# A two-layer diffusion step on one core: filter products over all 128 rows, two sample tiles routed by pairs, sample rows squared ahead

## What is computed

```python
def _rmsnorm(x, g):
    return x * rsqrt(mean(x * x, axis=-1) + EPS) * g

h = _rmsnorm(x, norm_mix) * (1 + scale1) + shift1        # first norm of a layer

f = sin(z @ w1 + b1); f = sin(f @ w2 + b2)               # implicit filters
h = (f @ w3)                                             # w3 has 64 rows
filt = h * exp(-decay * t)

q = (h2 @ wq)                                            # 8 heads, two halves each
s = einsum(q, sub_keys)                                  # 128 scores for each half
s1, i1 = top_k(s[:, :, 0], 16); s2, i2 = top_k(s[:, :, 1], 16)
cand = s1[..., :, None] + s2[..., None, :]               # routing
top, pos = top_k(cand, 16); g = softmax(top)
a = gelu(einsum('td,thkd->thk', h2, u_tab[idx]))         # 128 experts for each row
x = x + gate2 * einsum('thk,thkd->td', a * g, v_tab[idx])
```

## Time and profile before

| what | us |
|---|---|
| median of 3 runs | 4684.39 |
| the three runs | 4674.54 to 4685.51 |
| the profiled execution's own time | 4676.89 |
| its span | 4675.1 |

### The profile page before, as it was taken

The page is one execution under the profiler, slowest core; times in us unless marked ns, Lnnn a source line. Parts: engine busy times, 40 slices in busy tenths (PEclk is TensorE's granted clock), DMA queues, the critical chain, the costliest instruction groups (busy, mean ns, idle before and its releaser), DMA issues.

```text
span 4675.1 us, 42187 instructions
## 1 busy us (share of the span) xinstructions
PE 3775.7 (81%) x12598; PEld 2021.8 (43%) x12598; DVE 3207.1 (69%) x7383; ACT 1562.2 (33%) x4531; POOL 2083.7 (45%) x1769
## 2 busy tenths in 40 slices
PE   7988799897897877757867789999698777777776
PEld 4547574446453333324533356446554232332222
DVE  1322878887888876766567778977798866755554
ACT  2321341001344444434334333100234444444444
POOL 2240355573344434454444455565244444444443
PEclk8889899998899998988999899999899899899999
DMA  7655478896899989999999777877699999999998
GB/s 278 203 203 221 178 243 299 309 348 227 330 419 401 406 364 402 417 412 386 390 420 421 299 276 271 318 279 270 268 412 409 388 410 422 408 417 421 422 421 346
DMA packets 268416, 1604.74 MB, mean 343 GB/s; under 512 B 31686, under 2 KB 34034, under 8 KB 112540
## 3 DMA queue, kind: packets, MB, share of 16 engines
q0 software_dynamic: 234880, 1395.89, 75.3%
q1 hardware_dynamic: 33308, 206.16, 11.3%
HBM read 1590.62 MB, written 11.30 MB: 343 GB/s over the span
## 4 chain that ended last, share of the span: by engine, by line
PE 31%; DMA 30%; DVE 23%; issue 6%; POOL 5%; ACT 5%; SPq 0%; DVEq 0%; ACTq 0%; POOLq 0%
DMA sb_arena<-in_peer_uv,sb_idx 15%; PE ps L1166 12%; DMA sb_gbufs<-in_peer_uv,sb_idx 11%; DVE sb_gbufs L1990 4%; PE ps L1062 3%; PE ps L1103 3%; DVE sb_arena L1990 3%; DVE sb_eacc L2015 3%; POOL sb_gbufs L2239 3%; PE ps L1080 1%; DMA sb_gbufs<-in_peer_uv,sb_idx_v 1%; DVE sb_arena L1972 1%; DMA sb_ring<-in_w_oab 1%; PE ps L735 1%; DVE sb_arena L1974 1%
## 5 line engine op out<-in xcount | busy, mean ns | idle before, releaser
L1166 PE MATMUL ps<-sb_gbufs,sb_dge 128*128 128x512 f32 x1836 | 911.4, 646 | 286.4 <-ACT sb_dge L1473 282.0
L1166 PE MATMUL ps<-sb_arena,sb_dge 128*128 128x512 f32 x1832 | 882.8, 631 | 254.4 <-ACT sb_dge L1473 254.4
L2253 POOL DMA_INDIRECT sb_gbufs<-in_peer_uv,sb_idx x512 | 618.9, 1209 | 891.0 <-PE ps L1166 738.1
L2253 POOL DMA_INDIRECT sb_arena<-in_peer_uv,sb_idx x512 | 615.2, 1201 | 749.8 <-PE ps L1166 648.2
L1990 DVE CUSTOM_DVE_ANT_0 sb_gbufs<-sb_gbufs,sb_keep 128x1024 f32<-128x1024 f32 x512 | 625.6, 1234 | 372.7 <-DMA sb_gbufs<-in_peer_uv,sb_idx 370.9
L1990 DVE CUSTOM_DVE_ANT_0 sb_arena<-sb_arena,sb_keep 128x1024 f32<-128x1024 f32 x512 | 622.7, 1229 | 344.2 <-DMA sb_arena<-in_peer_uv,sb_idx 342.0
L1166 PEld LDWEIGHTS ps<-sb_gbufs,sb_dge 128*128 128x128 f32 x1836 | 362.3, 206 | 799.6 <-ACT sb_dge L1473 401.8
L1166 PEld LDWEIGHTS ps<-sb_arena,sb_dge 128*128 128x128 f32 x1832 | 353.0, 200 | 750.9 <-ACT sb_dge L1473 375.6
L1449 ACT ACTIVATE sb_small<-sb_small 128x2 f32<-128x2 f32 x512 | 104.1, 203 | 1502.3 <-DVE sb_small L1990 1498.8
L2239 POOL DMA_INDIRECT sb_gbufs<-in_peer_uv,sb_idx x256 | 317.8, 1241 | 305.3 <-DVE sb_small L1990 114.4
L2239 POOL DMA_INDIRECT sb_gbufs<-in_peer_uv,sb_idx_v x256 | 341.0, 1332 | 248.1 <-DVE sb_eacc L2015 182.2
(11 more groups left out here) (279 smaller groups left out, 4291.0 us busy)
## 6 DMA issues: line engine op xcount, KB each, us to landing
sb_ring<-in_w_wq SPq DMA_DIRECT2D x48, 1024.0 KB, 7.3
sb_keep<-in_w_ada POOLq DMA_DIRECT2D x52, 512.0 KB, 6.2
sb_ring<-in_w_hy SPq DMA_DIRECT2D x24, 1024.0 KB, 8.1
sb_ring<-in_w_oab SPq DMA_DIRECT2D x18, 1024.0 KB, 8.2
sb_ring<-in_w_ga SPq DMA_DIRECT2D x16, 1024.0 KB, 7.2
sb_ring<-in_w_gb SPq DMA_DIRECT2D x16, 1024.0 KB, 8.2
sb_ring<-in_w_out SPq DMA_DIRECT2D x14, 1024.0 KB, 8.5
sb_gbufs<-in_peer_uv,sb_idx POOLq DMA_INDIRECT x768, 11.1
```

The costliest lines, as they stand in the source:

```text
L1166: q = pe.matmul(ps[:, c, :], dge[:, b, :], gbuf[b][:, D + c * 512:D + c * 512 + 512], start=(h == 0 and i == 0), stop=(h == HALVES - 1 and ...
L2253: nc.gpsimd.indirect_dma_start(out=gbuf[b], out_offset=None, in_=I["peer_uv"], in_offset=bass.IndirectOffsetOnAxis(ap=idx[:, n + SLOTS:n + ...
```

## The change

The edits, in the order of the running kernel:

1. **Filter products.** `w3` and `f2T` are taken with 128 rows in place of 64. DVE clears rows 64 to 127 of both once, at the very start, and the filter pass waits for that.
2. **Squares ahead.** Layer 0's sample rows are squared by ACT beside the prompt's query points 10 to 13 of phase 0, and their roots are made by DVE at the end of phase 0. Layer 1's are squared in layer 0's token stage, two steps into the next tile, except for the last tile, which is squared at the start of layer 1; the roots are made there.
3. **A diagonal in place of scaled rows.** For the samples DVE writes four 128 x 128 diagonals of roots (in place of four scaled tiles), and PE multiplies `x` by them (`matmul`, in place of `transpose`).
4. **One more prompt point.** The prompt's squares and scaled rows are a point of their own, with nothing on PE. All P points go ahead of tokens on PE. The token from which P is handed out (`first`) moves from 43 to 51.
5. **Routing by pairs in two pieces.** `route_heads` gives way once, after `places`. Tiles 1 and 2 are both routed so; tile 1 has six R1 pieces (three pairs), tile 2 eight (four pairs).
6. **The order.** 10 tokens stand beside tile 1's queries (5 before). The 16 other query points stand beside tokens 10 to 25 (5 to 20 before), and the tokens with a DVE sum move with them. The R pieces follow from token 26. The double piece goes. In layer 1 the pieces come with each token up to token 35 and then with every second.

```diff
-        order += ["G"] + ["D"] * 4 + ["V", "R1"] + ["D"] * 4 + ["V", "V", "R1"] + ["D"] * 4 + ["V", "V", "R1", "D"]
+        order += ["G"] + ["D"] * 4 + ["R1", "V", "R1", "V"] + ["D", "D", "V"] * 2 + ["R1", "V", "R1", "V"]
+        order += ["D", "D", "V"] * 2 + ["R1", "V", "R1", "V", "D"]
...
-        points, given, first, last = (len(GR[0].pace()) if more else 0), 0, TOKENS + 11, TOKENS_S - 10
-        for m in range(5, TOKENS_S + 1):
+        points, given, first, last = (len(GR[0].pace()) if more else 0), 0, TOKENS + 19, TOKENS_S - 10
+        for m in range(FIRST_QUERY, TOKENS_S + 1):
...
-            elif between and (more or m < TOKENS or m % 3 == 0):
+            elif between and (more or m < TOKENS + 4 or m % 2 == 0):
                 order.append(between.pop(0))
-                if m == first and between:
-                    order.append(between.pop(0))
...
-        if name == "D" and at or name == "P" and at and point not in BEHIND:
+        if name in "DP" and at:
...
+                        if g.latent:
+                            m = pe.matmul(to, x[:, g.t0 + j, c * 128:c * 128 + 128], dge[:, j, :], start=True, stop=True)
...
-                        pe.matmul(ps[:, i % 2, :], Filters.f2T[:, i // 2 * 128:i // 2 * 128 + 128], Filters.w3[:, (i % 2) * HYW:(i % 2 + 1) * HYW],
+                        pe.matmul(ps[:, i % 2, :], Filters.f2T_all[:, i // 2 * 128:i // 2 * 128 + 128], Filters.w3_all[:, (i % 2) * HYW:(i % 2 + 1) * HYW],
...
+            def square_of_row(layer, t):
+
+                if layer:
+                    act.wait_ge(Z["x_done"], t)
+                if t > 1:
+                    act.wait_ge(Z["row_sq"], (TILES - 1) * layer + t - 1)
+                act.activation(hT[:, SQUARES:SQUARES + D], x[:, t, :], ACT.Square, accum_out=st[:, 3 + t:4 + t]).then_inc(Z["row_sq"], 1)
...
+                    for j in range(nt):
+                        dve.tensor_scalar(dge[:, j, :], ident[:, :], st[:, 36 + j:37 + j], None, ALU.mult).then_inc(s["xn"], 1)
...
-                if n < SLOTS and n % 32 == 0:
-                    pool.wait_ge(Z["gw1"], 4 * layer + n // 32 + 1)
+                if tile in BY_PAIRS and n % 32 == 0:
+                    pool.wait_ge(Z["gw1"], pairs_before(tile, layer) + n % SLOTS // 32 + 1)
```

More of the change, by code:

```diff
@@ L289, with pairs_before, routed_before @@
 PAIR_HEADS = 2
+SQUARES, SQUARES_AT = 2560, NHP - 6
+BY_PAIRS = (1, 2)
+FIRST_PAIR = {1: len(INLINE), 2: 0}
+def pairs_before(tile, layer):
+    return PH // PAIR_HEADS * (len(BY_PAIRS) * layer + BY_PAIRS.index(tile))
+def routed_before(tile, layer):
+    return (TILES - len(BY_PAIRS)) * layer + (tile - len(BY_PAIRS) if tile else 0)
 MERGED_BY_VECTOR = 7
@@ L1173, in route @@
             def route(tile, layer):
-                for _ in range(PH // PAIR_HEADS - len(INLINE) if tile == 1 else PIECES):
+                for _ in range(2 * (PH // PAIR_HEADS - FIRST_PAIR[tile]) if tile in BY_PAIRS else PIECES):
                     yield
@@ L1205, in dense @@
                     act.wait_ge(Z["rest"], 16 * 5)
-                if d == 1:
-                    act.wait_ge(Z["x_in"], 16)
                 if not g.latent and layer:
                     act.wait_ge(Z["px"], layer)
-                for j in range(nt):
-                    act.activation(v.xn[:, j, :], x[:, g.t0 + j, :], ACT.Square, accum_out=st[:, j:j + 1]).then_inc(s["ss1"], 1)
+                if not g.latent:
+                    act.activation(v.xn[:, 0, :], x[:, 0, :], ACT.Square, accum_out=st[:, 0:1]).then_inc(s["ss1"], 1)
+                elif layer:
+                    square_of_row(layer, nt)
+                if not g.latent:
+                    yield
                 act.wait_ge(Z["mod"], 9 if layer else 2)
@@ L1482, in expert_step, with pair_weights @@
                 yield
-            def pair_weights(layer, pair):
-                act.wait_ge(Z["top1"], PH // PAIR_HEADS * layer + pair + 1)
+            def pair_weights(layer, pair, tile=1):
+                act.wait_ge(Z["top1"], pairs_before(tile, layer) + pair + 1)
                 act.activation(inline["gex"], inline["gex"], ACT.Exp).then_inc(Z["ge1"], 1)
             def route(tile, layer):
-                if tile == 1:
-                    for pair in range(len(INLINE), PH // PAIR_HEADS):
-                        pair_weights(layer, pair)
+                if tile in BY_PAIRS:
+                    for pair in range(FIRST_PAIR[tile], PH // PAIR_HEADS):
+                        pair_weights(layer, pair, tile)
+                        yield
                         yield
@@ L1874, in dense @@
                             best_sixteen(p, i - 1)
+                        if d == 0 and i == NHP:
+                            dve.wait_ge(Z["row_sq"], TILES - 1)
+                            roots_of_rows()
                         if g.latent and p == 0 and i in INLINE:
-                            route_heads(layer, INLINE[i])
+                            for _ in route_heads(layer, INLINE[i]):
+                                pass
                         yield
@@ L1946, in route_heads @@
                 weights_of(mem, gwt[:, at:at + 32].rearrange("p (h k) -> p h k", h=PAIR_HEADS), PAIR_HEADS, 0.5 / GELU_C).then_inc(Z["gw1"], 1)
+                yield
             def route(tile, layer):
-                if tile == 1:
-                    for pair in range(len(INLINE), PH // PAIR_HEADS):
-                        route_heads(layer, pair)
-                        yield
+                if tile in BY_PAIRS:
+                    for pair in range(FIRST_PAIR[tile], PH // PAIR_HEADS):
+                        yield from route_heads(layer, pair, tile)
                     return
@@ L2126, in dense @@
                 s, v, at, nt, T = S, views[g.name], counted(d), g.nt, g.T
-                for _ in range(1 + nt + 1 + nt + 2 + nt * NH + 1):
+                for _ in range(1 + nt + 1 + nt + 2 + nt * NH + 1 + (not g.latent)):
                     yield
@@ L2243, in gather @@
                 b, tile = SLOT["s", layer, n][0], 1 + n // SLOTS
-                if n < SLOTS and n % 32 == 0:
-                    pool.wait_ge(Z["gw1"], 4 * layer + n // 32 + 1)
-                if n >= SLOTS and n % SLOTS == 0:
-                    pool.wait_ge(Z["gw"], 4 * layer + tile)
+                if tile in BY_PAIRS and n % 32 == 0:
+                    pool.wait_ge(Z["gw1"], pairs_before(tile, layer) + n % SLOTS // 32 + 1)
+                if tile not in BY_PAIRS and n % SLOTS == 0:
+                    pool.wait_ge(Z["gw"], routed_before(tile, layer) + 1)
                 if n == 4:
```

71 lines of the change are left out of this document (45 added, 26 removed).

## The result

The changed kernel takes **4634.04 us** in the median of 4 runs (4631.91 to 4640.58), against 4684.95 for the kernel before on the same chip (4 runs, 4674.54 to 4689.18). The ratio is 0.9902, with a 95% interval of 0.988 to 0.9924. The forecast was 4619 and the range 4570 to 4655, so it is faster as forecast, by less. The profiled execution is the longest of the four (4640.58), and the one before was a short one (4676.89), so the spans differ by 36 us where the medians differ by 51.

The account below looks back on a forecast made before the run. PE and its waits bound phase 0 and the dense stages; gather bytes plus DMA holes bound token stages. Terms -18 - 4 - 37 - 6 + 4 + 3 = -58 took the profiled 4676.9 us to 4619, range 4570 to 4655.

Parts of the forecast that it names:

- filter products: Phase 0's filter passes: products over 128 rows keep PE's clock high, -18 us, between 0 and -34.
- starts: Start of the samples' dense part, both layers: squares ahead and diagonals save 5.2 and 6.5, products cost 3.9 each; net -4.
- first ten tokens, both layers: Tokens beside tile 1's queries: ten take 128 us instead of 147, -19 in layer 0 and -18 in layer 1.
- double piece: Layer 0, before token 44: without two routing pieces together, half of PE's 12.07 us wait is gained, -6 (0 to -12).
- tile 2 by pairs: Token stages: routing tile 2 by pairs puts DVE later, +2 us for each layer, +4 (0 to +11).
- denser points: Layer 0's tokens: phase 1's prompt points go into 67 tokens in place of 75, +3 us (-5 to +8).
- first rival: Phase 0: the clock doesn't follow rows, so wider filter products gain nothing; 4637 us, chance 0.17.
- no 12 us wait of PE before the prompt's points: Sign of being right, layer 0's tokens: PE's 12.07 us wait for weights at token 44 goes.
- first tokens slower: Tokens beside tile 1's queries: held by DVE or PE at 1.2 GHz, gaining only 8 us per layer; 4640, chance 0.12.
- the hole only moves: Token stages: the loss of the first 105 us returns beside the 16 later query points; 4656, chance 0.05.
- the slower one: Tokens beside tile 1's queries keep 19.4 us each in one serial loop, +47 per layer; 4750, chance 0.03.
- Everything at its good bound: Whole kernel: terms at -34, -4, -49, -12, 0, 0; 4578 us, chance 0.08.

## Why the prediction was right, and where its sizes were off

Term by term, in us (negative is faster):

| term | forecast | measured | by |
|---|---|---|---|
| filter products | -18 | -12.6 inside the change, -22 alone | medians |
| starts | -4 | -3.7 - 2.6 = -6.3 | PE's rows |
| first ten tokens, both layers | -37 | -30.8 | medians |
| double piece | -6 | +4.6 (-2 to +7), with the prompt's first turns moved ahead | medians, ratio's interval |
| tile 2 by pairs | +4 | +0.7 | medians |
| denser points | +3 | +7.6 | medians |
| sum | -58 | -37, or -46 with the -22 | |
| whole | -58 | -51, -44 in its repeat | medians |

- *Filter products.* "I take -18, nearer to the products' own price" held within its range. The first rival, no help from the clock, falls: taking the rows away costs 12.6 us. PE was busy with 64 rows too, 57.56 of the 65 us around the fourth pass, at a clock of 0.64. The Trainium skill (TensorE: Matmul & The Clock Gate, Part 1) ties the clock to how busy PE has been and doesn't speak of rows. Read as busy time, it has the wider products bring nothing, and the runs disagree. But my reason was too simple as well. The first pass, one of the two I counted, was fast in the changed kernel with 64 rows too (one profile), so the point that moved the filters probably frees it as well, which I had costed at nothing for the clock. That would make the term smaller inside the change than alone, as the medians have it.
- *Starts.* The gains of 6.5 and 5.2 measured 12.82 - 6.61 = 6.2 and 13.91 - 8.98 = 4.9. The products gave back 2.5 and 2.4 of it, where I had 3.9 each, because ACT's last copy, part of both forms, ends sooner behind them (1.07 us in place of 1.77 and 1.30) and the turns, at 5.64 and 6.59, took longer than half of 8.85; they ran at a clock of 0.63 and 0.52, where the 3.9 was worked out for the high level.
- *First tokens.* "Get 128: -19 in layer 0 and -18 in layer 1": ten tokens take 129.1 and 130.3, and the lead is 17.9 and 16.9 where tile 2 begins. That these agree so well is luck: one step was wrong, and another wrong step made up for it. Today's ten tokens take 155.7 and not 147, since the next five don't run at 9.95 us beside queries. So the lead at the tenth token is 26.6 (26.3 in layer 1), of which 8.7 (9.4) goes by tile 2's first gather. From the one gather to the other a token takes 11.4 and 11.2 us, where it took 11.0 and 10.7. The rate there is the old one (415 GB/s against 414), so nothing stalls. The five query loads of half a megabyte that used to stand among tokens 5 to 9 come there now, 6 us at that rate; this part is argued from the order, not tried.
- *Double piece.* The wait for token 44's weights did go with it (3.55 us are left), but a new one of 11 to 14 us came in, and no run has the one without the other. The step that failed is one that the sum doesn't have. All P points go ahead of tokens on PE, which I costed at nothing, and so the prompt's first turns hold up a token's products: 12.12 us in the changed kernel, where I had said "no 12 us wait of PE before the prompt's points". What a kernel without the double piece and with these turns behind the token would take stays open.
- *Tile 2 by pairs.* Too small to see in time. But the new order of layer 1's pieces had a cost I hadn't placed: some of them moved onto the change of tile, where they met the finished rows of the output on DVE, which the prediction left out.
- *Denser points.* The term was mis-sized, 3 for 7.6; a share of today's loss in proportion to the density was too little. In the changed kernel slices 16 to 20 lose 38 us against the 28 before, just under the 40 that I had named as a sign of being wrong.

Of the rivals, *first tokens slower* and *the hole only moves* don't hold, nor does the slower one: a token beside tile 1's queries takes 12.9 us, well under 15.8. *Everything at its good bound* was added up wrongly: it has -4 for the starts and 0 for the points, where their own good bounds are -12 and -5. Of what would show it, the start 5 us behind the meeting, 64 records, over 380 GB/s in the first 105 us and ten tokens in 128 came true within 3 us; the second and fourth pass near 8 us, the clock above 0.9 in the fourth's window and no 12 us wait did not. One sign of being wrong did appear: tokens 10 to 25 slower than 11 us each, by the 11.4 and 11.2 above.

## To carry to other kernels

When gathers bound a stage and buffers come free by another engine's products, put those products ahead of unrelated work in that engine's order: this was some two thirds of the gain. When an edit is to take away a wait, read that stretch of the timeline again afterwards, behind it and in front of it: here a wait of the same length came in for another reason. Where one engine has fixed extra work at known tokens (here a finished tile), keep optional work off them: moving it gave another 6.5 us.

## What the runs showed of the hardware

- The slow passes of 64 row products ran in windows with a clock of 0.60 to 0.66, with PE hardly idle. The same products over 128 rows, half of them zeros, had 0.81 to 1.00 in all four passes. The fourth pass took 14.9 to 15.1 us in four profiles with 64 rows and 9.0 to 11.0 in ten with 128. Zeros bought 12.6 us in the median.
- Whether 64 row products are slow also depends on what runs between them: the first pass took 13.3 us in three executions and 7.9 in a fourth, with the filters one prompt point earlier against the prompt's work.
- Two executions of one kernel were 14 us apart by layer 0's first sample gather and within 4 us in each later stage. Of the 14, 9 were there at the prompt's first gather (518.93 and 528.01).
